# A hybrid encoder trunk with routed experts: another expert goes first, and the router works in unsplit float32

## The reference

```python
def moe_swiglu(x, router_w, router_b, wg, wu, wd):        # cut
    logits = xt.astype(F32) @ router_w.astype(F32) + router_b.astype(F32)
    top_logit, top_idx = lax.top_k(logits, TOP_K)          # 2 of 8 experts per token
    top_w = jax.nn.softmax(top_logit, axis=-1)
    ...
    def expert_block(args):                                # rows of one expert
        tok, w, e = args
        xb = xt[tok]
        h = jax.nn.silu(xb @ wg[e]) * (xb @ wu[e])
        return (h @ wd[e]).astype(F32) * w[:, None]
    ...
    out = jnp.zeros((n_tok, D), F32).at[row_tok].add(y.reshape(n_rows, D))
```

## Time and profile before

| | |
|---|---|
| median of three runs | 1170.74 us |
| profiled execution | 1171.44 us |
| its span (first to last instruction) | 1169.0 us |
| TensorE busy | 1126.1 us (96%) |
| VectorE busy | 669.3 us (57%) |
| ScalarE busy | 542.4 us (46%) |
| GpSimd busy | 77.9 us (7%) |
| read from memory | 375.77 MB, 322 GB/s over the span |

### The profile page before, as it was taken

One profiled execution on the slowest core, in us unless ns is written; L12 is line 12 of the kernel. 1 busy time (PEld: TensorE's weight loads), 2 busy tenths in 40 slices (PEclk: granted clock), 3 DMA queues, 4 the chain that ended last, 5 costly groups with the idle time before them and its releaser, 6 DMA issues.

```text
span 1169.0 us, 16635 instructions
## 1 busy us (share of the span) xinstructions
PE 1126.1 (96%) x6525; PEld 834.4 (71%) x6525; DVE 669.3 (57%) x934; ACT 542.4 (46%) x840; POOL 77.9 (7%) x101
## 2 busy tenths in 40 slices
PE   8998999999999998999999999999999999999995
PEld 7976888887897887855688755688755788655441
DVE  6788545455777897810698710898610998411104
ACT  4774444444486675610676610776401876301002
POOL 0001000001000396000000000000000000000001
PEclk8998999999999999999999999999999999999998
DMA  9833554554434198989999999999899999899994
GB/s 385 358 131 145 227 204 171 200 182 144 165 115 181 75 371 339 365 348 421 421 421 420 380 405 420 420 422 421 356 422 420 420 421 420 353 422 420 421 420 176
DMA packets 52764, 377.88 MB, mean 323 GB/s; under 512 B 5888, under 2 KB 6016, under 8 KB 7120
## 3 DMA queue, kind: packets, MB, share of 16 engines
q1 hardware_dynamic: 51408, 370.69, 78.7%
q0 software_dynamic: 992, 5.56, 1.3%
q10 hardware_dynamic: 288, 0.59, 0.1%
HBM read 375.77 MB, written 1.05 MB: 322 GB/s over the span
## 4 chain that ended last, share of the span: by engine, by line
PE 78%; DVE 7%; DMA 5%; ACT 4%; POOL 4%; issue 1%; DVEq 0%; ACTq 0%; SPq 0%; POOLq 0%
PE bank L813 15%; PE bank L563 11%; PE bank L565 11%; PE bank L564 10%; PE bank L804 7%; PE bank L715 5%; PE bank L718 5%; PE bank L721 5%; DMA raw<-W 4%; PE bank L790 3%; DVE wlo L1592 2%; PE bank L736 1%; PE bank L557 1%; PE bank L875 1%; PE bank L795 1%
## 5 line engine op out<-in xcount | busy, mean ns | idle before, releaser
L1592 DVE TENSOR_TENSOR wlo<-raw,whi 128x1024 fp32r<-128x1024 f32 x260 | 305.5, 1229 | 18.6 <-ACT whi L1145 17.7
L1145 ACT ACTIVATE whi<-raw 128x1024 fp32r<-128x1024 f32 x260 | 255.4, 1051 | 0.0
L565 PE MATMUL bank<-whi,al 128*128 128x512 f32 (+1 forms) x624 | 235.1, 377 | 0.0
L813 PE MATMUL bank<-raw,xg 128*64 128x256 f32 x1760 | 205.4, 383 | 2.8 <-DMA raw<-W 2.6
L1644 DVE TENSOR_TENSOR he<-he,bank 128x128 f32<-128x128 f32 x55 | 15.8, 288 | 289.3 <-ACT he L1200 289.3
L813 PEld LDWEIGHTS bank<-raw,xg 128*64 128x64 f32 x1760 | 120.2, 137 | 67.8 <-DMA raw<-W 6.1
L1270 DVE TENSOR_TENSOR wlo<-raw,whi 128x1024 fp32r<-128x1024 f32 x110 | 130.4, 1222 | 27.7 <-ACT whi L964 26.9
L563 PE MATMUL bank<-whi,xgh 128*128 128x512 f32 x352 | 142.7, 405 | 2.7 <-DVE wlo L1592 2.5
L564 PE MATMUL bank<-wlo,xgh 128*128 128x512 f32 x352 | 137.1, 390 | 0.0
L565 PEld LDWEIGHTS bank<-whi,al 128*128 128x128 f32 x624 | 118.8, 190 | 22.2
L964 ACT ACTIVATE whi<-raw 128x1024 fp32r<-128x1024 f32 x114 | 115.3, 1057 | 23.3 <-PE bank L565 17.5
(11 more groups left out here) (285 smaller groups left out, 1434.0 us busy)
## 6 DMA issues: line engine op xcount, KB each, us to landing
raw<-W SPq DMA_DIRECT2D x352, 1024.0 KB, 12.2
scr<-gb_d POOLq DMA_DIRECT2D x3, 1024.0 KB, 5.1
scr<-wbd_d POOLq DMA_DIRECT2D x2, 512.0 KB, 6.2
x<-gb_d POOLq DMA_DIRECT2D x1, 1024.0 KB, 8.2
out_d<-acc SPq DMA_DIRECT2D x4, 256.0 KB, 2.0
x<-x_d SPq DMA_DIRECT2D x1, 512.0 KB, 4.0
x<-x_d ACTq DMA_DIRECT2D x1, 512.0 KB, 8.7
rtab<-rt_d POOLq DMA_DIRECT2D x1, 228.0 KB, 2.8
```

The lines of the kernel that those rows point to most:

```text
L565: return nc.tensor.matmul(out, sl, mh, start=False, stop=last, skip_group_check=True)
L813: last = nc.tensor.matmul(bank[n * NARROW:(n + 1) * NARROW, c % 2, 0:FC].rearrange("p (a n) -> p a n", a=2), xg[:, kk, :], gu[:, :, n * P: ...
L1145: nc.scalar.activation(whi[:, q % SPLIT, h * HW:(h + 1) * HW], raw[:, i % RING, h * HW:(h + 1) * HW], ACT.Copy).then_inc(hi_rdy, 1)
L1592: V.tensor_tensor(wlo[:, q % SPLIT, h * HW:(h + 1) * HW], raw[:, i % RING, h * HW:(h + 1) * HW], whi[:, q % SPLIT, h * HW:(h + 1) * HW].bi ...
```

## The change

Three things at once. The expert that is forced to rank 0 and fetched ahead is the last, 7, instead of 0. The router's logits come from x transposed and kept whole in `xT`: sixteen float32 matmuls with tokens on partitions, so nothing is turned afterwards; `rw2`, `xnh` and `xnl` go, and the gathers read x itself and an S of float32. The fillers ahead of the logits go from 9 to 2, and in the first job `S` and the gathers move to later steps. The last norm's scale gets a buffer of its own. The diff, cut:

```diff
+FIRST = NE - 1
+FIRST_S_AT = 22
+FIRST_GATHER_AFTER = {25: 0, 28: 1}
-WARM = {..., "split": 9, "rank": 10, "slots": 5}
+WARM = {..., "split": 2, "rank": 10, "slots": 5}
-        S = sb("S", [P, NT, P], F32R)
+        S = sb("S", [P, NT, P])
+        xT = sb("xT", [P, KT, T])
-        xnh = sb("xnh", [P, NT, D], F32R)
-        xnl = sb("xnl", [P, NT, D], F32R)
+        gbx = sb("gbx", [P, 2, D])
...
-                    sp.dma_start(raw[:, s, :], W[STREAM + m]).then_inc(raw_in[s], 16)
+                    sp.dma_start(raw[:, s, :], W[STREAM + FIRST * FFP + m]).then_inc(raw_in[s], 16)
...
-                link(G.tensor_scalar(key[:, 0:1], key[:, 0:1], 1.0e5, None, ALU.add))
+                link(G.tensor_scalar(key[:, FIRST:FIRST + 1], key[:, FIRST:FIRST + 1], 1.0e5, None, ALU.add))
... gather
-                    for n, (t, a) in enumerate(((0, xnh), (0, xnl), (1, xnh), (1, xnl))):
-                        last = nc.tensor.matmul(bank[:, 4 + b, k * P:k * P + m], a[:, t, kk * P:(kk + 1) * P],
-                                                S[:, t, 0:m], start=(n == 0), stop=(n == 3))
+                    for t in range(NT):
+                        last = nc.tensor.matmul(bank[:, 4 + b, k * P:k * P + m], x[:, t, kk * P:(kk + 1) * P],
+                                                S[:, t, 0:m], start=(t == 0), stop=(t == NT - 1))
... between
-                if i in GATHER_AFTER:
+                halves = FIRST_GATHER_AFTER if first else GATHER_AFTER
+                if i in halves:
... router
-                split_ready(3, 1, 1)
-                pe.wait_ge(rw_l, 1)
-                for k in range(KT):
-                    nc.tensor.matmul(bank[0:2 * NE, 2, 0:T], rw2[:, k].rearrange("p a e -> p (a e)"), xTh[:, k, :], ...)
-                    last = nc.tensor.matmul(bank[0:NE, 2, 0:T], rw2[:, k, 0, :], xTl[:, k, :], ...)
-                last.then_inc(lgT_ps, 1)
-                pe.wait_ge(lgT_sb, 1)
-                for t in range(NT):
-                    nc.tensor.transpose(...).then_inc(lg_ps, 1)
+                pe.wait_ge(rt_in, 16)
+                for t in range(NT):
+                    for g in range(2):
+                        pe.wait_ge(xTb_rdy if g else xTa_rdy, t + 1)
+                        for k in range(4 * g, 4 * g + 4):
+                            last = nc.tensor.matmul(bank[:, 3, (3 + t) * NE:(4 + t) * NE], xT[:, k, t * P:(t + 1) * P],
+                                                    rw[:, k * NE:(k + 1) * NE], start=k == 0, stop=k == KT - 1)
+                    last.then_inc(lg_ps, 1)
... ScalarE, norm before the router
-                        act.wait_ge(x_rdy, 2 * (2 * NT + t + 1))
-                        nc.scalar.activation(xnh[:, t, :], x[:, t, :], ACT.Copy).then_inc(xn_h, 1)
+                        act.wait_ge(xT_ps, 12 + 2 * t + 1)
+                        nc.scalar.activation(xT[:, 0:4, t * P:(t + 1) * P], bank[:, xbank(t, 0), :]..., ACT.Copy
+                                             ).then_inc(xTa_rdy, 1)
... mixer: the router weights' split goes, on ScalarE and VectorE
-                    dve.wait_ge(rw_h, 1)
-                    V.tensor_tensor(rw2[:, :, 1, :], ..., ALU.subtract).then_inc(rw_l, 1)
... VectorE, the low halves of x become one copy per tile
+            def copy_x(t):
+                dve.wait_ge(xT_ps, 12 + 2 * t + 2)
+                V.tensor_copy(xT[:, 4:8, t * P:(t + 1) * P], bank[:, xbank(t, 1), :]...).then_inc(xTb_rdy, 1)
... VectorE, first job
-                    if i == S_AT:
+                    if i == (FIRST_S_AT if first else S_AT):
-            one_hot([ps_e[:, t, 0:1] for t in range(NT)], WIDE)
+            one_hot([ps_e[:, t, FIRST:FIRST + 1] for t in range(NT)], WIDE)
```

More of the change, by code:

```diff
@@ L89, in piece_of @@
     return CLASSES[J], J // 2, i
-WARM = {"start": 8, "mixer": 2, "dense": 12, "last_mixer": 18, "tile": 20, "split": 9, "rank": 10, "slots": 5}
+WARM = {"start": 8, "mixer": 2, "dense": 12, "last_mixer": 18, "tile": 20, "split": 2, "rank": 10, "slots": 5}
 POOL_PIECES = (MIXP + 1, MIXP + FFP + 1)
@@ L832, in between @@
                     for t in range(NT):
-                        last = nc.tensor.transpose(bank[0:n, 7, t * P:(t + 1) * P], S[:, t, 0:n].bitcast(F32), ident[:])
+                        last = nc.tensor.transpose(bank[0:n, 7, t * P:(t + 1) * P], S[:, t, 0:n], ident[:])
                     last.then_inc(st_ps, 1)
-                if i in GATHER_AFTER:
+                halves = FIRST_GATHER_AFTER if first else GATHER_AFTER
+                if i in halves:
                     if not first:
@@ L838, in between @@
                     pe.wait_ge(S_rdy, J + 2)
-                    gather(GATHER_AFTER[i], WIDE if wide_after else NARROW)
+                    gather(halves[i], WIDE if wide_after else NARROW)
             def wide_job(J, n, first):
@@ L901, in router @@
                 keep_warm(WARM["split"], 3, htl[:, :, :].rearrange("p t n -> p (t n)"))
-                split_ready(3, 1, 1)
-                pe.wait_ge(rw_l, 1)
-                for k in range(KT):
-                    nc.tensor.matmul(bank[0:2 * NE, 2, 0:T], rw2[:, k].rearrange("p a e -> p (a e)"), xTh[:, k, :],
-                                     start=k == 0, stop=False, skip_group_check=True)
-                    last = nc.tensor.matmul(bank[0:NE, 2, 0:T], rw2[:, k, 0, :], xTl[:, k, :], start=False,
-                                            stop=k == KT - 1, skip_group_check=True)
-                last.then_inc(lgT_ps, 1)
-                pe.wait_ge(lgT_sb, 1)
-                for t in range(NT):
-                    nc.tensor.transpose(bank[:, 3, 3 * NE + 2 * t * NE:3 * NE + 2 * (t + 1) * NE],
-                                        lgs[0:2 * NE, t * P:(t + 1) * P], ident[0:2 * NE, 0:2 * NE]).then_inc(lg_ps, 1)
+                pe.wait_ge(rt_in, 16)
+                for t in range(NT):
+                    for g in range(2):
[4 more added lines that the diff above has]
+                    last.then_inc(lg_ps, 1)
                 keep_warm(WARM["rank"], 4)
@@ L984, in std @@
                     nc.scalar.activation(rstd[:, t:t + 1], mv[:, t, 1:2], ACT.Sqrt).then_inc(std_rdy, 1)
-                    if split:
+                    if split and ph < 2:
                         split_x(ph + 1, t)
                     if ph == 2:
-                        act.wait_ge(x_rdy, 2 * (2 * NT + t + 1))
-                        nc.scalar.activation(xnh[:, t, :], x[:, t, :], ACT.Copy).then_inc(xn_h, 1)
+                        act.wait_ge(xT_ps, 12 + 2 * t + 1)
+                        nc.scalar.activation(xT[:, 0:4, t * P:(t + 1) * P],
+                                             bank[:, xbank(t, 0), :].rearrange("p (k t) -> p k t", k=4),
+                                             ACT.Copy).then_inc(xTa_rdy, 1)
             def mixer(l):
@@ L1344, in norm @@
                 scale(1)
-                if ph == 2:
-                    split_x(ph + 1, 0)
-                split_x(ph + 1, 1)
-                if ph == 2:
+                if ph < 2:
+                    split_x(ph + 1, 1)
+                else:
                     for t in range(NT):
-                        low_x(t)
+                        copy_x(t)
             def softplus():
```

32 lines of the change are left out of this document (7 added, 25 removed).

## The result

The changed kernel takes 1093.8 us (median of 4 runs, 1091.67 to 1094.61); the kernel before took 1170.33 us beside it (4 runs, 1169.42 to 1171.97). The ratio is 0.934 with a 95% interval of 0.9325 to 0.9359: 76.5 us less. The forecast was 1089, with 1085 to 1095 for 8 in 10: the sign is right, the time lies inside the range but outside the main case (1086.5 to 1092), 4.8 us above the forecast. That it lies inside the range is in part luck: the upper end was drawn for a lower clock in the router and for late tables, and most of the loss came from elsewhere. The profiled execution took 1094.61 us, with a span of 1092.8.

A forecast was written before the change was run, and what follows sets the result against it. TensorE was taken to bound the kernel, waiting for weights only in the extra job. -77.0 - 3.9 - 1.0 = -81.9 us from 1171.44 gave 1089.5, 1088.8 as median, stated as 1089; 8-in-10 range 1085 to 1095.

The forecast's parts named there:

- main case: Whole kernel: the forecast without any rival coming true, 1086.5 to 1092 us, given 82%.
- late tables: First job: GpSimd slower by 12 us more, so the matrix at step 22 waits some 3 us; 1092 us, 4%.
- The extra job: After the eighth job: with expert 7 first no expert overflows, the extra narrow job goes, -77.0 us.
- The jump over the loop: Behind the eighth job: engines jump over the extra-job loop; queued matmuls cover it, 0 us, +2 for the range.
- The slot table: First job: matrix moved from step 14 to 22, so TensorE's 3.88 us stall behind GpSimd's tables goes fully, -3.9 us.
- Norm and router: Between second mixer and first job: transposes, fewer fillers and float32 logits together, -1.0 us.
- transposes: Router, both tiles: an earlier x saves only what the transposes waited, -0.3 us.
- fillers and logits: Router: seven fillers fewer, -1.6 us; float32 logits replacing float32r logits, copy and small transposes, +0.9 us.
- the rival with the clock: Router: seven fillers fewer and 3.5 us of 8-column matmuls lower TensorE's clock, +4 us, so 1093; 8%.
- Gathers: Gather halves in the jobs: 8 float32 matmuls for 16 float32r, same records, 0 us; upper end +37 us.
- an unchanged count: Extra job: one token's choice changed by rounding puts expert 2 at 65 rows and the job returns; 1166 us, 2%.
- two extra jobs: End of the jobs: two narrow experts over 64 rows give two extra jobs; 1253 us, 1%.

The follow-up runs named there:

- first-expert kernel: The kernel before with only the expert that goes first changed, 7 for 0; old router, gathers and slot table kept: 1097.03 us, ratio 0.9383.
- its own experiment: The changed kernel with the first job's one-hot matrix back at step 14 and its gathers after steps 17 and 20: 1098.31 us, ratio 0.9384.
- nine fillers: The changed kernel with 9 instead of 2 filler matmuls ahead of the logits: 1095.74 us, ratio 0.9361.
- 1086.8: The changed kernel with TensorE's last scatter also written ahead of the jump, and 2 and 18 fillers around the transposes for 18 and 20: 1086.79 us, ratio 0.9284.

## Why the prediction was right, and where it was off

**The extra job (-77.0).** Right in every step: counts of 319 and 44, and 77.0 us gone from the chain. The eighth job kept its time, 68.5 us for 68.4.

**The jump over the loop (0 kept, up to +2).** This term failed. Two mistakes are in it. The choice: 0 was taken because 2.7 us of queued matmuls lie over the reading of the count. They do cover it, but the instructions behind the jump then come another 1.8 us late (2.69 in the first-expert kernel), 4.1 to 5.0 us behind the count's reading in all. The Trainium skill ("Runtime: NRT & Kernel Launch", Instruction fetch mechanics) says that a taken branch to a target outside the fetched window waits for a DMA; the trace agrees, as the gap exists only where the loop is jumped (1.80 to 2.69 us) and not where it is entered (0.14), though no row shows the fetch itself. The upper end: +2 counted the gap alone. Behind a standing TensorE came the lower clock (the scatter's first half +1.26) and, behind the slow scatter, a slower addition on VectorE (+0.85), so the price was 3.8. Fillers in front of the jump take back the latter two, the scatter in front of it all three.

**The slot table (-3.9).** Right in mechanism, too small by about 1 us: 5.0 by its own experiment. The step that failed reads TensorE's two long gaps (2.95 + 0.93) as the price. They are its lower end: behind them the splits come one by one, TensorE's matmuls last longer or, in three of the four kernels with this wait, run at a lower clock, and all of this counts as busy. The execution from which the price was read was the one without the lower clock. The job got 4.73 us shorter, its idle time 3.86, its busy time 0.90. The table itself was late as forecast, and a little later, 457.9 for 454, since GpSimd's small operations took 1.1 to 1.4 us beside the splits.

**Norm and router (-1.0).** Measured +0.5. By its terms: transposes -0.45 (forecast -0.3), fillers and logits 3.93 us for 4.68, -0.75 (forecast -0.7), so the durations were right. What turned the sign is the rival with the clock, +1.34 on the ten fillers and about +0.3 on the rest up to the first job. The rival was priced at +4 and given 8%; it came true at some 40% of its price, for the clock is back at 1.00 after 395 us. Its own condition, some 8 us of work at half speed, would have cost 8 and not 4, so the price was a slip that lay nearer to the truth by chance. That 1093.8 is near the 1093 of this rival is chance too: the end lost more than the router. It names the right place, but its cause (seven fillers fewer) is refuted by nine fillers, and its other half (3.5 us of 8-column matmuls) holds.

**Gathers (0).** 1.98 us where the same half took 1.93 with the old form, and 0.5 us more over jobs 2 to 8. The bound of +37 was far too wide; 0 was the right choice.

**Late tables, an unchanged count, two extra jobs.** None occurred: no wait at step 22, 319 pieces.

**The sum.** -81.9 became -76.2 of span: +3.8 at the end, +1.5 router, +0.5 gathers, +0.7 ahead of the change, -0.8 slot table. The profiled execution lies 1.8 us over its span and 2.4 before, which leaves +5.1 of execution, 1094.61 for 1089.5.

**What stays open.** Why the gap differs between 1.80 and 2.69 us, and when the clock falls behind it. In the six kernels that jump without fillers in front, the whole scatter took 4.95 to 6.78 us for 3.67. In two of them (the first-expert one and the one with the slot matrix at step 14) the first half still took 1.97 us and the clock fell in the second; in the others the first half took 2.3 to 3.4. Whether the old router, its weight split moved behind the norm so that fewer fillers pay, would beat 1086.8 wasn't tried.

## What to carry to other kernels

A loop that usually runs zero times isn't free: put what is urgent ahead of the jump, even at the price of writing it twice. When an edit frees an engine in front of a row of fillers, change their counts in the same edit, or the gain stays inside them. Price a removed stall by the length of the whole stage until work flows as usual again, not by the idle time on the engine that is last: it can be busy and slow.

## What the runs showed of the hardware

- A jump over the loop's body on TensorE: the first matmul behind it starts 4.1 to 5.0 us after the count was read (seven kernels); with the last matmuls above it 1.80 to 2.69 us of "issue" remained, 0.85 with eight fillers more.
- TensorE can be busy 5.00 of 5 us and be granted 0.66 (in one kernel 0.50 over 5 us) behind 3.5 to 4.2 us of float32 matmuls that move 8 columns. With a 512-column matmul after every four records it was granted 1.00.
- A filler of 512 columns, 0.23 us in a row of its like, takes 0.33 us among such matmuls, and a float32 logit matmul 0.17 us there (0.34 for four records) instead of 0.22 alone.
- VectorE's first addition of the end (128x512) took 1.83 us in the timeline where GpSimd's addition ran beside it for 1.25, and 0.99 where it did for 0.44. Less the overlap it is 0.55 to 0.58 us in five kernels, as if VectorE's stood still while GpSimd's ran. That is an estimate, since it was never seen without any overlap.
- After 2.95 us of standing in the first job the granted clock stayed at 1.00 (the kernel before); after 2.96 us it was 0.54 over the next 3.6 us (slot matrix back at step 14), and after 3.98 us 0.50 from 446 to 450 us (the kernel before with fewer fillers).
